# The order of VectorE's work in the attention heads of a two-block transformer kernel

## The chip, the cores and the metric

The kernel runs on one core of one Trainium2 chip. The metric is the device time of one execution in microseconds (us), as a median of several runs. All arithmetic is in 32-bit floats. TensorE (PE) does the matrix products and transposes, VectorE (DVE) and ScalarE (ACT) the elementwise work, SyncE (SP) starts nearly all transfers, GpSimd (POOL) a few gathers and scatters at the end.

## The reference, cut to what matters

Two transformer blocks run one after the other on 512 tokens of width 1024. The first block is a feed-forward part, a mixer with 16 attention heads of width 64, and a second feed-forward part. The second block has a gated linear attention, a latent attention and a mixture of 64 experts. The change touches only the 16 heads of the first block's mixer: eight "stick-breaking" heads, then eight "forgetting" heads.

```python
z = einsum('bhqd,bhkd->bhqk', q, k) * scale                 # stick-breaking
log_keep = where(mask, log_sigmoid(-z), 0.0)
later = cumsum(log_keep, axis=3, reverse=True) - log_keep
w = where(mask, exp(log_sigmoid(z) + later), 0.0)

fq, fk = rms_norm(fox_q, g_q), rms_norm(fox_k, g_k)         # forgetting, per head
z = einsum('bhqd,bhkd->bhqk', fq, fk) * scale + log_f_cum_q - log_f_cum_k
p = softmax(where(causal mask, z, -inf), axis=-1)

out = w @ v   or   p @ v;   mixer output = heads @ w_o
```

## The kernel before, in words

Every engine has its own written-out program, and semaphores tie them together; there is no planner. Each engine works its instructions off in the order in which they are written, so an instruction whose wait isn't met holds back everything behind it on that engine. What follows is the stretch of the mixer (about 590 to 890 us of the profiled execution).

The 16 heads (h = 0 to 15) come in 8 pairs (p = h // 2). Pairs 0 to 3 are stick-breaking, pairs 4 to 7 forgetting. n = h + 1 is the next head. While head h is turned and multiplied with its values, the scores and weights of head n are made, and the projections of a later pair run on PE.

PE, for each head h: `turn(h)` transposes the weights of the head (10 tiles of 128 x 128, line 800) once they are there (`s_p`). `scores(h + 1)` makes the next head's scores in PSUM banks 0 to 2 (line 791); in a forgetting pair it waits for the normed queries and keys of the pair (`s_qn`). `head_out(h)` multiplies the turned weights with the values into bank 6 (line 818); it waits for both copies of the turned tiles. Then comes projection work. In an odd head it is `first_half(p + 2)`: queries and keys of pair p + 2 (line 767), and for a forgetting pair the sum of squares of the queries (line 840). In an even head it is `second_half(p + 1)`: for a forgetting pair the sum of squares of the keys (line 848), and then `values(p + 1)` into bank 6 (line 773). `values` may only start when VectorE has copied the head's output out of bank 6 (`s_o`). In heads 13 and 14 six blocks of the output projection (`mix`, line 858) take that place.

ScalarE, for each head: a copy of six turned tiles (line 1331), then the exponentials of the next head, `softplus_log` and `stick_weights` or `forget_exp` (line 1316, one activation for each of four row tiles, each as soon as its maximum is there), and the copies and square roots of the projections (`raw_out`, `deviation`, line 1299). The root of the queries of pair p + 1 comes at the end of the odd head before (it ends up beside the turn of head h), the root of its keys in the even head h itself.

VectorE, for each head (lines 1679 to 1708):

- `turned_out(h)`, lines 1640 and 1643: the copy of four turned tiles, which waits for the turn.
- `head_copy(h)`, line 1647: bank 6 to SBUF, which waits for `head_out(h)` (`s_pv`).
- `log_weights(n)`, lines 1609 to 1617: for a stick-breaking head n. It waits for ScalarE's logarithm, and its last step releases ScalarE's exponential, which releases `turn(n)`.
- `masked_max(n)`, lines 1624 and 1627: for a forgetting head n, four additions of the mask and four row maxima, each of which releases one activation on ScalarE.
- `forget_probs(n)`, lines 1631 and 1634: waits for the four activations, then a reciprocal and four scalings; releases `turn(n)`.
- `inverse(p + 1, m)`, line 1651: the reciprocal of the deviation of the queries (m = 0) or keys (m = 1), in place; waits for ScalarE's root.
- `normed(p + 1, m)`, line 1658: two products, one for each head of the pair; releases `scores` through `s_qn`.
- `forget_rows`, lines 1665 and 1667: extra rows of queries and keys, in odd heads.
- `mix_part(d)`, line 1672: in heads 13 and 14, adds a block of the output projection to the residual.

The two inversions and the two norms stand in the even heads 6, 8, 10 and 12 (pairs 4, 5, 6 and 7). Head 6 is even too, but its next head, 7, is still stick-breaking: there the order is head copy, `log_weights(7)`, `inverse(4, 0)`, `normed(4, 0)`, `inverse(4, 1)`, `normed(4, 1)`. In heads 8, 10 and 12 it is `inverse(p + 1, 0)`, `masked_max(n)`, head copy, `forget_probs(n)`, `normed(p + 1, 0)`, `inverse(p + 1, 1)`, `normed(p + 1, 1)`.

Of the kernel before, what the change touches and what calls it, by code (L numbers as in the profile page):

```python
# [131 lines left out]
def build(nc, a, out):  # L132
    ctx = ExitStack()
    with ctx:
# [20 lines left out]
        def const(name):  # L155
            at, n = CONST[name]
            return cst[:, at:at + n]

        def col(name, j=None):
            at, n = COLS[name]  # L160
            return cols[:, at:at + n] if j is None else cols[:, at + j:at + j + 1]
# [25 lines left out]
        N_PAIR = 8  # L187
# [254 lines left out]
        def unit_psum(n):  # L442
            b = 2 * (n % 4)
            _, _, m, wide, _ = UNITS[n]
            return ps[0:m, b:b + 2, 0:TOK // 2] if wide else ps[0:m, b, :]
# [199 lines left out]
        def _(pe):  # L645
# [272 lines left out]
            for n, (it, c0, m, wide, _) in enumerate(UNITS):  # L918
                if it != item:
                    if item >= 0:  # L920
                        pe.drain().then_inc(freed[2 + item], 1)
                    item = it
                    pe.wait_ge(filled[2 + it], u.take(2 + it, 1)[0] + 16)
                if n >= 4:

                    pe.wait_ge(s_p2c[n % 2], (n - 4) // 2 + 1)
                b = 2 * (n % 4)
                for k in range(KC):
                    if n == 0:
                        pe.wait_ge(s_hn, KC * 3 + k + 1)  # L930
                    flags = dict(start=(k == 0), stop=(k == KC - 1))
                    if wide is None:
                        t = n - 4
                        last = mm(ps[0:m, b, :], hT[:, k, TILE0[t]:TILE0[t] + m], w2(it)[:, k, :], **flags)
                    elif wide:
                        for g in range(2):
                            last = mm(ps[0:m, b + g, 0:264], w2(it)[:, k, c0:c0 + m], hT[:, k, g * 264:(g + 1) * 264], **flags)
                    else:
                        last = mm(ps[0:m, b, :], w2(it)[:, k, c0:c0 + m], hT[:, k, META:TOK], **flags)
                last.then_inc(s_p2, 1)  # L940
# [538 lines left out]
        def _(dve):  # L1479
# [5 lines left out]
            def link(ins):  # L1485

                ins.then_inc(vec_sem[0], 1)
                steps[0] += 1
                dve.wait_ge(vec_sem[0], steps[0])
# [114 lines left out]
            def z_tiles():  # L1604
                return [ps[:, b, at:at + P * (t + 1)] for t, (b, at) in enumerate(Z_AT)]

            def log_weights(h):
                dve.wait_ge(s_sp, h + 1)
                v.scalar_tensor_tensor(out=buf1[:, 0:768].rearrange("p (b n) -> p b n", b=2), in0=ps[:, 0:2, 0:384],
                                       scalar=0.0, in1=buf1[:, 0:768].rearrange("p (b n) -> p b n", b=2),  # L1610
                                       op0=ALU.max, op1=ALU.add)
                link(v.scalar_tensor_tensor(out=buf1[:, 768:TRI], in0=ps[:, 2, :], scalar=0.0, in1=buf1[:, 768:TRI],
                                            op0=ALU.max, op1=ALU.add))
                link(v.tensor_tensor_scan(buf2[:, ::-1], const("resets")[:, ::-1], buf1[:, ::-1], 0.0, ALU.mult, ALU.add))
                v.tensor_tensor(buf1[:, 0:768].rearrange("p (b n) -> p b n", b=2), ps[:, 0:2, 0:384],
                                buf2[:, 0:768].rearrange("p (b n) -> p b n", b=2), ALU.subtract)
                v.tensor_tensor(buf1[:, 768:TRI], ps[:, 2, :], buf2[:, 768:TRI], ALU.subtract).then_inc(s_zz, 1)

            def masked_max(h):
                dve.wait_ge(s_z, h + 1)  # L1620
                tiles = z_tiles()
                for t in (3, 2, 1, 0):
                    diag = tiles[t][:, t * P:(t + 1) * P]
                    last = v.tensor_tensor(diag, diag, const("after"), ALU.add)
                link(last)
                for t in (3, 2, 1, 0):
                    v.tensor_reduce(fox_s[:, t:t + 1], tiles[t], AX_X, ALU.max, negate=True).then_inc(s_mx, 1)

            def forget_probs(h):
                dve.wait_ge(s_e, 4 * (h - 7))  # L1630
                link(v.reciprocal(fox_s[:, 8:12], fox_s[:, 4:8]))
                for t in range(4):
                    b = buf2[:, TILE_AT[t]:TILE_AT[t] + P * (t + 1)]
                    last = v.tensor_scalar(b, b, fox_s[:, 8 + t:9 + t], None, ALU.mult)
                last.then_inc(s_p, 1)

            def turned_out(h):
                dve.wait_ge(s_pt, h + 1)
                if h < 8:
                    v.tensor_tensor(PT[:, 0:4, :], ps[:, 3, :].rearrange("p (b q) -> p b q", b=4),  # L1640
                                    const("strict_t").unsqueeze(1).to_broadcast([P, 4, P]), ALU.mult).then_inc(s_ptc, 1)
                else:
                    v.tensor_copy(PT[:, 0:4, :].rearrange("p b q -> p (b q)"), ps[:, 3, :]).then_inc(s_ptc, 1)

            def head_copy(h):
                dve.wait_ge(s_pv, h + 1)
                v.tensor_copy(oT[h % 2 * HD:(h % 2 + 1) * HD, h // 2:h // 2 + 1, :], ps[0:HD, 6:7, :]).then_inc(s_o, 1)  # L1647

            def inverse(p, m):
                dve.wait_ge(s_qstd, 2 * (p - 4) + m + 1)  # L1650
                link(v.reciprocal(eb[:, m, :], eb[:, m, :]))

            def normed(p, m):
                dve.wait_ge((s_qc, s_kc)[m], p + 1)
                g = (gqs[:, p - 4:p - 3], col("g_k", p - 4))[m]
                for hh in range(2):
                    rows = slice(hh * HD, (hh + 1) * HD)
                    last = v.scalar_tensor_tensor(out=(qF, kF)[m][p % 2][hh][0:HD, :], in0=raw[m][rows, :], scalar=g[rows, :],
                                                  in1=eb[rows, m, :], op0=ALU.mult, op1=ALU.mult)
                last.then_inc(s_qn, 1)  # L1660

            def forget_rows(p):
                if p < 6:
                    for hh in range(2):
                        v.memset(qF[p % 2][hh][HD:72, :], 1.0)
                for hh in range(2):
                    v.tensor_scalar(kF[p % 2][hh][HD:72, :], Fc, ident[0:8, 2 * (p - 4) + hh:2 * (p - 4) + hh + 1], None, ALU.mult)\
                        .then_inc(s_fm, 1)

            def mix_part(d):  # L1670
                dve.wait_ge(s_wo, d + 1)
                v.scalar_tensor_tensor(out=xT[:, d, META:TOK], in0=ps[:, 7 - (d % 3) % 2, :], scalar=gate[1][:, d:d + 1],
                                       in1=xT[:, d, META:TOK], op0=ALU.mult, op1=ALU.add).then_inc(s_wp, 1)
# [5 lines left out]
            for h in range(N_HEAD):  # L1679
                p, n = h // 2, h + 1  # L1680
                turned_out(h)
                if n < 8:
                    head_copy(h)
                    log_weights(n)
                if h % 2 == 0 and 4 <= p + 1 < N_PAIR:
                    inverse(p + 1, 0)
                if n >= 8:
                    if n < N_HEAD:
                        masked_max(n)
                    head_copy(h)  # L1690
                    if n < N_HEAD:
                        forget_probs(n)
                if h == 0:
                    dve.wait_ge(s_f1, 2)
                    link(v.scalar_tensor_tensor(out=fA, in0=fA, scalar=0.0, in1=fB, op0=ALU.max, op1=ALU.add))
                    link(v.memset(fB, 1.0))

                    link(v.tensor_tensor_scan(Fc, fB, fA, 0.0, ALU.mult, ALU.add))
                if h % 2 == 0 and 4 <= p + 1 < N_PAIR:
                    normed(p + 1, 0)  # L1700
                    inverse(p + 1, 1)
                    normed(p + 1, 1)
                if h % 2 and 4 <= p + 2 < N_PAIR:
                    forget_rows(p + 2)
                if h in (13, 14):
                    for d in range(3 * (h - 13), 3 * (h - 13) + 3):
                        mix_part(d)
# [14 lines left out]
            for n in range(0, len(UNITS), 2):  # L1722
# [5 lines left out]
                if n - 1 in GATE_PAIRS:  # L1728

                    h = GATE_PAIRS[n - 1]  # L1730
# [110 lines left out]
            for un in range(GH * NT):  # L1841
                h, t = un // NT, un % NT
# [248 lines left out]
```

## Time and profile before

| | |
|---|---|
| three runs | 2852.21, 2854.35, 2855.42 us; median 2854.35 us |
| the profiled execution | 2856.67 us, of which span 2854.9 us |
| mean granted TensorE clock | 0.939 of full speed |
| PE busy | 2518.7 us (88%) |
| DVE busy | 1047.9 us (37%) |
| ACT busy | 465.7 us (16%) |
| POOL busy | 179.6 us (6%) |
| DMA | 563.19 MB, mean 197 GB/s |

The span runs from the first to the last instruction. Busy shares are of the span; weight loads of PE overlap its products and are counted apart. The granted clock is the share of TensorE's full speed that the chip gave it; 1.00 is 2.4 GHz and 0.50 is 1.2 GHz. In the page's 40 slices the stretch of the heads is slices 9 to 12, where PE is at nine tenths or more in each slice, VectorE at three to five tenths.

### The profile page before, as it was taken

The page shows a single profiled execution, that of the slowest core. Times are in us where ns is not written, and L with a number is a line of the kernel's source. Part 1 is how long each engine was busy: PE and PEld are TensorE (multiplying, and loading weights), DVE is VectorE, ACT ScalarE, POOL GpSimd, SP SyncE. Part 2 cuts the span into 40 slices and gives each one's busy share as a digit, 9 for nine tenths or more (in the row PEclk, how much of TensorE's full clock was granted, in tenths as well). Part 3 has the DMA queues.
Part 4 walks back from the last instruction along what each step waited for, and adds up shares of the span by engine and source line. Part 5 has one row for each costly group of instructions (what it writes and reads, how often), then busy time and mean ns, then how long its engine had stood idle before and what let it go on. Part 6 is the DMA issues. An engine that isn't in the chain of part 4 may idle for free. (4 is left out here: it accounts for less than half of the span.)

```text
span 2854.9 us, 24606 instructions
## 1 busy us (share of the span) xinstructions
PE 2518.7 (88%) x9051; PEld 1170.1 (41%) x9051; DVE 1047.9 (37%) x1236; ACT 465.7 (16%) x732; POOL 179.6 (6%) x458
## 2 busy tenths in 40 slices
PE   8999999999998999999997798688888788878884
PEld 4444444465564444434444454333333233323331
DVE  3655530145462333310106633433333333333334
ACT  2000000155332000000102130011111111111111
POOL 0000000000000000000000000111111111111110
PEclk9999999999899999999998799799899989999997
DMA  7444534122101121413201000799999999999995
GB/s 269 147 147 147 175 129 105 33 51 61 49 1 59 59 88 59 120 41 90 86 19 64 0 8 30 310 413 417 411 412 407 411 406 404 410 405 413 403 413 222
DMA packets 182831, 563.19 MB, mean 197 GB/s; under 512 B 16864, under 2 KB 132848, under 8 KB 156544
## 3 DMA queue, kind: packets, MB, share of 16 engines
q1 hardware_dynamic: 172384, 554.10, 50.8%
q0 software_dynamic: 10400, 8.42, 1.0%
q8 instruction: 35, 0.57, 0.1%
q14 instruction: 12, 0.10, 0.0%
HBM read 567.19 MB, written 20.97 MB: 206 GB/s over the span
## 5 line engine op out<-in xcount | busy, mean ns | idle before, releaser
L1143 PE MATMUL ps<-slot,xT 128*64 128x512 f32 x2048 | 516.4, 663 | 164.6 <-DMA slot<-in_expert_w_up 163.9
L715 PE MATMUL ps<-hT,slot 128*128 128x512 f32 x1408 | 614.4, 597 | 13.0 <-ACT hT L1238 7.2
L715 PEld LDWEIGHTS ps<-hT,slot 128*128 128x128 f32 x1408 | 267.9, 192 | 351.0 <-issue 347.4
L1143 PEld LDWEIGHTS ps<-slot,xT 128*64 128x64 f32 x2048 | 155.6, 152 | 523.5 <-issue 304.5
L743 PE MATMUL ps<-big,slot 128*128 128x512 f32 x704 | 310.4, 601 | 12.0 <-DVE big L1565 6.2
L1974 DVE COPY hT<-ps 128x256 f32<-128x256 f32 x64 | 27.2, 425 | 632.0 <-PE ps L1151 632.0
L1162 PE MATMUL ps<-slot,hT 128*64 128x512 f32 x1024 | 235.6, 602 | 1.2 <-DVE hT L1974 1.2
L1965 DVE RECIPROCAL xT<-xT 64x512 f32<-64x512 f32 x64 | 214.1, 3345 | 2.2
L743 PEld LDWEIGHTS ps<-big,slot 128*128 128x128 f32 x704 | 135.7, 193 | 182.0 <-issue 169.0
L1561 DVE RECIPROCAL eb<-eb 128x512 f32<-128x512 f32 x44 | 147.5, 3353 | 1.5
L1559 DVE TENSOR_SCALAR eb<-eb 128x512 f32<-128x512 f32 x44 | 18.8, 427 | 331.8 <-ACT eb L1248 331.8
L1444 ACT ACTIVATE xT<-ps 64x512 f32<-64x512 f32 x64 | 37.8, 590 | 599.4 <-PE ps L1143 599.4
L1588 DVE SCALAR_TENSOR_TENSOR xT<-ps,small,xT 128x512 f32<-128x512 f32 x16 | 12.0, 751 | 296.5 <-PE ps L743 296.5
L1162 PEld LDWEIGHTS ps<-slot,hT 128*64 128x64 f32 x1024 | 68.8, 137 | 116.1 <-issue 111.9
L2028 POOL MEMSET spare<- 1x4 f32 x1 | 0.1, 91 | 1806.7 <-DVEq L463 1806.7
L1450 ACT ACTIVATE hT<-ps 64x512 f32<-64x512 f32 x128 | 75.7, 592 | 203.1 <-PE ps L1162 202.4
L767 PE MATMUL ps<-hT,slot 128*128 128x512 f32 x240 | 105.9, 597 | 0.0
L1248 ACT ACTIVATE eb<-ps 128x512 f32<-128x512 f32 x44 | 26.3, 597 | 419.4 <-PE ps L715 419.3
L1225 ACT ACTIVATE tmp<-xT 128x512 f32<-128x512 f32 (+1 forms) x32 | 20.1, 632 | 368.0 <-DVE xT L1588 327.9
L1125 PE MATMUL ps<-cst,xT 64*128 64x64 f32 x512 | 67.1, 272 | 7.5 <-DMA xT<-normed_tokens,tcol 7.5
L773 PE MATMUL ps<-slot,hT 128*128 128x128 f32 x512 | 61.8, 284 | 6.9 <-DVE big L1647 6.9
L767 PEld LDWEIGHTS ps<-hT,slot 128*128 128x128 f32 x240 | 44.8, 190 | 55.1 <-issue 55.1
(331 smaller groups left out, 2313.2 us busy)
## 6 DMA issues: line engine op xcount, KB each, us to landing
slot<-in_expert_w_gate SPq DMA_DIRECT2D x64, 2048.0 KB, 19.4
slot<-in_expert_w_up SPq DMA_DIRECT2D x64, 2048.0 KB, 22.7
slot<-in_expert_w_down SPq DMA_DIRECT2D x64, 2048.0 KB, 25.0
slot<-in_w_mod SPq DMA_DIRECT2D x18, 2048.0 KB, 8.0
slot<-in_w_gate SPq DMA_DIRECT2D x22, 1024.0 KB, 5.5
slot<-in_w_up SPq DMA_DIRECT2D x22, 1024.0 KB, 7.9
slot<-in_w_down SPq DMA_DIRECT2D x16, 1408.0 KB, 7.4
slot<-in_w_in SPq DMA_DIRECT2D x24, 512.0 KB, 6.4
```

Of the source, the lines that this page charges most:

```text
L715: last = mm(ps[:, 2 * j + g, :], w[:, g, k, j * P:(j + 1) * P], hT[:, k, META:TOK], start=(k == 0), stop=(k == KC - 1))
L743: last = mm(ps[:, down_bank(d), :], w[:, f, :], aT[:, f, :], start=(f == 0), stop=(f == FC - 1))
L767: last = mm(ps[:, bank, :], pair_w[p][:, k, m, :], hT[:, k, META:TOK], start=(k == 0), stop=(k == KC - 1))
L773: last = mm(ps[:, bank, t * P:(t + 1) * P], hT[:, k, META + t * P:META + (t + 1) * P], pair_w[p][:, k, 2, :], start=(k == 0), stop=(k == K ...
L1125: last = nc.tensor.transpose(ps[:, 4 + j, k * CAP:(k + 1) * CAP], xs[j].rearrange("p (m k) -> p k m", k=KC)[:, k, :], ident[0:CAP, 0:CAP])
L1143: last = mm(ps[g * CAP:(g + 1) * CAP, j, :], xsT[j][:, k, :], w[g][:, k, :], start=(k == 0), stop=(k == KC - 1))
L1162: last = mm(ps[g * CAP:(g + 1) * CAP, 2 + j, :], hid[j][:, c, :], w[:, c, g * 512:(g + 1) * 512], start=(c == 0), stop=(c == 3))
L1444: av(sg[j], ps[0:CAP, j, :], ACT.Exp, scale=-1.0).then_inc(s_eg, 1)
L1450: last = av(ys[j][:, g * 512:(g + 1) * 512], ps[g * CAP:(g + 1) * CAP, 2 + j, :], ACT.Copy)
L1561: v.reciprocal(eb[:, j, :], eb[:, j, :]).then_inc(s_vec, 1)
L1965: v.reciprocal(sg[j], sg[j]).then_inc(s_vec, 1)
L1974: v.tensor_copy(hid[j].rearrange("p c s -> p (c s)"), ps[:, 6 + j, 0:4 * CAP]).then_inc(s_hd, 1)
```

## The change

In the loop over heads on VectorE, three things move. No instruction is added, dropped or resized, and the other engines' programs are the same.

1. In head 6, `inverse(4, 0)` and `normed(4, 0)` (one reciprocal and two products) are issued in front of `head_copy(6)` and `log_weights(7)`. They stood behind them.
2. In heads 8, 10, 12 and 14, `head_copy(h)` is issued in front of `masked_max(n)`. It stood between `masked_max(n)` and `forget_probs(n)`.
3. `inverse(p + 1, 0)` stands at the head of the loop body; in heads 8, 10 and 12 it is where it was, behind `turned_out(h)`.

Odd heads, and head 15, are as before.

```diff
             for h in range(N_HEAD):
                 p, n = h // 2, h + 1
                 turned_out(h)
+                if h % 2 == 0 and 4 <= p + 1 < N_PAIR:
+                    inverse(p + 1, 0)
+                if h == 6:
+                    normed(4, 0)
                 if n < 8:
                     head_copy(h)
                     log_weights(n)
-                if h % 2 == 0 and 4 <= p + 1 < N_PAIR:
-                    inverse(p + 1, 0)
-                if n >= 8:
+                elif h % 2 == 0:
+                    head_copy(h)
+                    masked_max(n)
+                    forget_probs(n)
+                else:
                     if n < N_HEAD:
                         masked_max(n)
                     head_copy(h)
...
                 if h % 2 == 0 and 4 <= p + 1 < N_PAIR:
-                    normed(p + 1, 0)
+                    if h != 6:
+                        normed(p + 1, 0)
                     inverse(p + 1, 1)
                     normed(p + 1, 1)
```

## Rows read from the trace of the kernel before

**Rows 1.** Waits of PE, 590 to 900 us: total us, times, longest.
```profile
PE ps L773 <- DVE big L1647: 6.9, 3, 2.3
PE ps L791 <- DVE slot L1658: 6.4, 1, 6.4
```

**Rows 2.** Timeline, heads 6 and 7: start, duration, engine, line, [idle before <- releaser].
```profile
692.55 0.69 ACT L1299 ACTIVATE eb<-ps,eps_col 128x512 f32<-128x512 f32 x1
...
696.79 0.68 DVE L1647 COPY big<-ps 64x512 f32<-64x512 f32 x1 [3.99 <-PE ps L818]
...
697.64 7.31 PE L773 MATMUL ps<-slot,hT 128*128 128x128 f32 x64
...
700.95 0.96 DVE L1609 SCALAR_TENSOR_TENSOR big<-ps,big 128x768 f32<-128x768 f32 x1 [3.49 <-ACT big L1306]
...
706.88 3.34 DVE L1651 RECIPROCAL eb<-eb 128x512 f32<-128x512 f32 x1
...
708.31 2.01 PE L800 MATMUL ps<-cst,big 128*128 128x128 f32 x10 [3.36 <-ACT big L1310]
...
715.18 1.51 DVE L1658 SCALAR_TENSOR_TENSOR slot<-tmp,cols,eb 64x512 f32<-64x512 f32 x2
...
716.74 4.64 PE L791 MATMUL ps<-slot 72*128 72x128 f32 x8 [6.42 <-DVE slot L1658]
...
721.31 4.53 PE L818 MATMUL ps<-big 128*64 128x128 f32 x20
```

**Rows 3.** Timeline, heads 8 and 9.
```profile
742.94 3.35 DVE L1651 RECIPROCAL eb<-eb 128x512 f32<-128x512 f32 x1 [0.48 <-ACT eb L1299]
...
743.82 2.40 PE L818 MATMUL ps<-big 128*64 128x128 f32 x20
...
746.15 1.13 PE L848 MATMUL ps<-eb,cst 128*128 128x512 f32 x2
746.32 0.89 DVE L1624 TENSOR_TENSOR ps<-ps,cst 128x128 f32<-128x128 f32 x4
...
748.85 0.67 DVE L1647 COPY big<-ps 64x512 f32<-64x512 f32 x1
...
749.58 9.04 PE L773 MATMUL ps<-slot,hT 128*128 128x128 f32 x64 [2.30 <-DVE big L1647]
...
756.48 1.51 DVE L1658 SCALAR_TENSOR_TENSOR slot<-tmp,cols,eb 64x512 f32<-64x512 f32 x2
...
759.87 2.32 PE L791 MATMUL ps<-slot 72*128 72x128 f32 x8
```

**Rows 4.** Timeline, heads 10 to 13.
```profile
788.24 7.41 PE L773 MATMUL ps<-slot,hT 128*128 128x128 f32 x64 [2.30 <-DVE big L1647]
...
795.14 1.51 DVE L1658 SCALAR_TENSOR_TENSOR slot<-tmp,cols,eb 64x512 f32<-64x512 f32 x2
...
796.90 2.33 PE L791 MATMUL ps<-slot 72*128 72x128 f32 x8
...
825.28 8.80 PE L773 MATMUL ps<-slot,hT 128*128 128x128 f32 x64 [2.30 <-DVE big L1647]
...
832.18 1.51 DVE L1658 SCALAR_TENSOR_TENSOR slot<-tmp,cols,eb 64x512 f32<-64x512 f32 x2
...
835.34 2.32 PE L791 MATMUL ps<-slot 72*128 72x128 f32 x8
```

**Rows 5.** Windows: length, busy of PE, PEld, DVE, ACT, POOL, then PEclk, DMA share, GB/s.
```profile
716.74:725.80 9.06, 9.06 (x29) 6.44 (x29) 3.25 (x9) 2.14 (x8) 0.00 (x0) 0.50 0.62 245
749.73:753.10 3.37, 3.37 (x17) 3.37 (x18) 2.87 (x8) 2.36 (x5) 0.00 (x0) 0.50 0.00 0
788.24:791.65 3.41, 3.41 (x30) 3.41 (x31) 2.78 (x7) 2.52 (x6) 0.00 (x0) 1.00 0.02 5
```

**Rows 6.** Timeline, head 14, PE and DVE.
```profile
856.00 10.57 PE L858 MATMUL ps<-big,slot 128*128 128x512 f32 x24
...
859.73 0.75 DVE L1672 SCALAR_TENSOR_TENSOR xT<-ps,small,xT 128x512 f32<-128x512 f32 x1 [0.64 <-PE ps L858]
```

## The prediction

> **What bounds the kernel now.** I read the page first. PE is busy for 88% of the span and VectorE for 37%, so as a whole VectorE sets nothing. But the change sits in the heads, and there the question is at which places PE stands still for VectorE. The page's chain of waits is of no use for that: it holds only the last steps of the kernel. The view that answers is PE's waits between 590 and 900 us. Two lines of it name VectorE: `values` (L773) waits three times for the head copy (L1647), 6.9 us in total, and `scores` (L791) waits once, 6.4 us, for a normed operand (L1658) [rows 1]. These are the four waits that the change aims at, 13.3 us in all. Then the timeline, to see what stands before each of them on VectorE.
>
> In heads 6 and 7 PE has finished `values(4)` at 697.64 + 7.31 = 704.95 us, waits 3.36 us for the last stick-breaking weights, turns them, and then waits 6.42 us until 716.74 for the normed keys of pair 4, which VectorE delivers at 715.18 + 1.51 = 716.69 [rows 2]. VectorE does two reciprocals and two norms in a row from 706.88 on, while before, until 696.79, it sat idle for 3.99 us.
>
> In heads 8, 10 and 12 PE stands for 2.30 us each before `values` [rows 3, 4]. In head 8 `head_out` ends at 743.82 + 2.40 = 746.22, yet the copy starts only at 748.85, because the mask and the maxima (from 746.32) are ahead of it. Everything PE does in this stretch outside the named waits is back to back, so a microsecond taken from PE's path here is one of the whole: what follows (feed-forward part, second block) starts from PE's end of it.
>
> The windows show a second price, the clock. PE ran at 0.50 (1.2 GHz) from 716.74 to 725.80, through all of `scores(8)` and `head_out(7)`, and for 3.4 us after the 2.3 us stop in head 8, but stayed at 1.00 (2.4 GHz) after the same stop in head 10 [rows 5]. Head 12's `values` took 8.80 us against 7.41 in head 10 [rows 4], so I read it as a fall too: two of three stops of 2.30 us were followed by the low clock.
>
> **Head 6: queries normed early.** Two instruction groups move from behind `log_weights(7)` to ahead of the head copy. `inverse(4, 0)` can start when ScalarE's root is there, 692.55 + 0.69 = 693.24; VectorE is free from 696.79 - 3.99 = 692.80. It ends at 693.24 + 3.34 = 696.58, the norm at 698.09, the head copy at 698.77 instead of 697.47 [rows 2]. So the copy is 1.3 us late and `values(4)` with it: it ends at 706.2 instead of 704.95. The cover is the 3.36 us wait for the stick-breaking weights, which arrive at 708.31 whatever PE does: `log_weights(7)` waits for ScalarE until 700.95 and VectorE is free at 698.8. Cost on the path: 0 (1.3 if that cover were gone). The SP queue refills a slot when `values(4)` ends, 1.3 us later, with weights that are used pairs later; no one waits for it.
>
> Behind the chain only the keys are left: 706.88 + 3.34 + 1.51 = 711.73, so `scores(8)` can start at 711.8 instead of 716.74. The turn of head 7 ends at 710.32, which is the next limit and lies below. Gain: 4.9 us. What is late next is still the normed keys, by 1.5 us. The clock is low there now and I expect it low again, since PE stands idle 2.1 us before the turn and 1.5 us behind it: 0 taken. Bounds: if it stays up, `scores(8)` and `head_out(7)` take 2.32 and 2.40 instead of 4.64 and 4.53 [rows 2, 3], 4.45 us more gain; if it rises later than now, up to 1 us is lost in the projection behind.
>
> **Heads 8, 10, 12: head copy first.** What goes: the 2.30 us before `values`. The copy can start at 746.3, when `head_out` has ended and `inverse(5, 0)` too (742.94 + 3.35 = 746.29), ends at 747.0, and PE is busy with L848 until 747.28 [rows 3]. So `values` starts without a stop, at 747.28. What is paid: the copy used to lie under ScalarE's exponentials; now mask, maxima, exponentials, scalings and the norms behind them all move back by its 0.67 us. The last of them releases the scores of the next head, and there the cover is thin:
>
> - Head 8: keys normed at 757.99 before, 758.66 now. The scores ran at 759.87 [rows 3]. They now start at 758.66: gain 1.21.
> - Head 10: keys normed at 796.65, now 797.32; scores at 796.90 before [rows 4]. Loss 0.42.
> - Head 12: 833.69, now 834.36; scores at 835.34 before. Gain 0.98.
>
> Sum 1.77 us of the 6.9 that seemed to be there. The rest becomes a new stop. With `values` at the full-clock 7.41 us, PE ends it in head 8 at 754.69. The turn in between takes 1.25 (before: end of `values` 758.62, scores 759.87), so PE could start the scores at 755.94 and stands until 758.66: 2.72 us. The same sum gives 2.72 in head 10 and 2.71 in head 12. VectorE is now the bound of the even heads.
>
> That new stop is longer than the 2.30 us ones and sits before `scores` and `head_out`, so a fall of the clock now costs there. No row shows this stop. Lower bound of its price: 0 per head. Upper bound: both instruction groups wholly at the low clock, 4.45 us, as in head 7 [rows 2]. A fall in `values` cost 9.04 - 7.41 = 1.63 and 8.80 - 7.41 = 1.39 us [rows 3, 4]. The rows nearest in kind are those of head 7, the nearest in length of stop are those of `values`; I take 2.5 us for each of three heads, 7.5 in all.
>
> The Trainium skill ("TensorE: Matmul & The Clock Gate", section "A second HAM failure mode: psum-queue depth-cycling") says that short pauses between groups of matmuls, met again at each turn through the PSUM banks, are enough to make the clock drop and recover over and over. It speaks against this change. By that rule all three new stops bring a fall; by this trace's two in three, two of them do: the sum at 2.5 each would be -0.8 or +1.7 us. The trace agrees that stops of 2.30 us suffice, though not each time.
>
> **Head 14.** The copy waits for `head_out(14)`, which ends at 856.0; before, mask and maxima went first. From the mask's start to the end of the probabilities is at most 757.99 - 746.32 - 1.51 - 3.35 - 1.51 = 5.3 us [rows 3], so they end by 856.7 + 5.3 = 862.0, under the 10.57 us of `mix`. `mix_part` (0.75) would end at 862.8; the third block of `mix`, which needs its bank, starts at 856.00 + 2/3 x 10.57 = 863.05 [rows 6]. Cost 0; 0.3 if that cover fails. The early `inverse` of point 3 of the change moves nothing in heads 8 to 12.
>
> **Sum.** 4.9 + 1.8 - 7.5 = -0.8, a loss of 0.8 us against the profiled execution: span 2854.9 + 0.8 = 2855.7, plus 1.8 around it, 2857.5. That execution lies 2.3 us above the median of the three runs, which spread over 3.2 us; on the median's scale the forecast is 2854.35 + 0.8 = 2855.2 us. What a measurement can tell from no change is about 0.2%, 5.7 us, so this is "the same".
>
> **Rivals.** (a) *The clock stays up.* If PE's new stops are not followed by low stretches, all 6.7 us are gained: 2847.7. With head 7's low stretch gone too, 2843.2. For it: head 10. Against it: heads 8 and 12, with shorter stops. Partly so (falls costing under 1 us in all) gives over 5.7 us. (b) *The new stop costs its full price*, the slower end. In heads 9, 11 and 13 scores and head output run wholly at 1.2 GHz: 3 x 4.45 = 13.35 against 6.7, so 6.65 us slower, 2861.0. It decides from 2.2 us a head on, where the gain is eaten; slower by over 0.2% it is from 4.1 us a head. For it: head 7, the one case in which this very pair of groups followed a wait for normed operands. Against it: the stop there was 6.42 us with another before it. By the skill's rule named above this is the case to expect. (c) *The copy is not the limit.* If `head_out` and `inverse` end later than the rows say, `values` still stands; then heads 8 to 12 give 1.77 less and only the stop moves, about 2849 to 2857. For it: copy and PE are within 0.1 us of each other. (d) *Head 6 pays.* The late `values(4)` reaches the turn: 1.3 of the 4.9 is lost, about 2856.5; the 2.1 us left speak against it.
>
> **How the numbers follow.** The forecast, with a clock price between 1 and 12.4 us in all, which takes in (c) and (d): 0.70, all within 0.2%. (a) 0.14, faster. (b) 0.16, slower. The range reaches from (a) without head 7, 2847.7, to (b), 2861.0, rounded outwards by half a microsecond for the spread of runs: 2847 to 2861.5. What is left out, clock up in head 7 as well or low longer than 4.45 us allows, and luck of the runs, I put at 0.18.
>
> **What would show it.** `scores(8)` starts about 15 us after the head output of head 6 has ended (696.8), not 20 as before. No wait of `values` for L1647 is left in heads 8 to 12; a new wait of L791 for L1658 of 2.7 us stands in heads 9, 11 and 13, and from the start of L848 to those scores it is 12.5 us in each. The window over scores and `head_out` there has a granted clock under 1.00. The forecast is wrong if those windows are at 1.00 throughout, or if L791's stops are short because the norms don't move back by 0.67.

## The result and the profile after

The changed kernel takes 2859.98 us (median of 22 runs, 2856.0 to 2862.96) against 2854.65 us before (22 runs, 2852.1 to 2857.45): ratio 1.0017, 95% interval 1.0011 to 1.0024. That is 5.3 us slower by the medians (the ratio makes it 4.9), just under the 0.2% (5.7 us) that I had called "the same", and it is a real difference: the interval leaves 1 out. The profiled execution has a span of 2856.2 us and a mean granted clock of 0.936.

Waits of PE after, 590 to 900 us (total us, times, longest), to be read against [rows 1]:

```profile
PE ps L791 <- DVE slot L1658: 9.8, 4, 2.7
PE ps L773 <- DVE big L1647: 1.0, 1, 1.0
```

The 6.9 us before `values` in heads 8, 10 and 12 are gone. Of the 6.4 us before `scores(8)`, 1.6 are left, but three new waits of 2.7 us stand in the same line.

Timeline after, heads 6 to 9 (start, duration, engine, line, [idle before <- releaser]), against [rows 2 to 4]:

```profile
690.78 1.02 PE L840 MATMUL ps<-eb,cst 128*128 128x512 f32 x2
...
699.65 7.41 PE L773 MATMUL ps<-slot,hT 128*128 128x128 f32 x64 [1.02 <-DVE big L1647]
709.14 1.94 PE L800 MATMUL ps<-cst,big 128*128 128x128 f32 x10 [2.08 <-ACT big L1310]
712.64 4.64 PE L791 MATMUL ps<-slot 72*128 72x128 f32 x8 [1.56 <-DVE slot L1658]
717.21 3.70 PE L818 MATMUL ps<-big 128*64 128x128 f32 x20
...
734.67 1.02 PE L840 MATMUL ps<-eb,cst 128*128 128x512 f32 x2
...
742.16 7.37 PE L773 MATMUL ps<-slot,hT 128*128 128x128 f32 x64
749.63 1.31 PE L800 MATMUL ps<-cst,big 128*128 128x128 f32 x10
753.69 4.34 PE L791 MATMUL ps<-slot 72*128 72x128 f32 x8 [2.75 <-DVE slot L1658]
```

VectorE in head 8 after: inverse, copy, mask, and the last norm (the maxima, probabilities and second inverse between them are left out):

```profile
737.99 3.35 DVE L1651 RECIPROCAL eb<-eb 128x512 f32<-128x512 f32 x1 [0.48 <-ACT eb L1299]
741.38 0.68 DVE L1647 COPY big<-ps 64x512 f32<-64x512 f32 x1
741.99 0.88 DVE L1624 TENSOR_TENSOR ps<-ps,cst 128x128 f32<-128x128 f32 x4
...
752.12 1.51 DVE L1658 SCALAR_TENSOR_TENSOR slot<-tmp,cols,eb 64x512 f32<-64x512 f32 x2
```

Windows after, over scores, head output and nothing else in heads 9 and 11; head 13 has the same (length, then busy of PE, PEld, DVE, ACT, POOL, then the granted clock, DMA share, GB/s):

```profile
753.69:761.68 7.99, 7.99 (x28) 5.52 (x28) 3.12 (x9) 1.96 (x8) 0.00 (x0) 0.57 0.00 0
794.53:802.53 8.00, 8.00 (x28) 5.55 (x28) 3.13 (x9) 2.08 (x8) 0.00 (x0) 0.57 0.00 0
```

PE never pauses in these windows and yet needs 8.0 us for what took 4.6 before (759.87 to 764.45). A granted clock of 0.57 means that most of that time it had 1.2 GHz.

To compare traces I use two distances. "Heads" is from the start of the last sum of squares before head 6 (L840, 690.78 here, 689.96 before) to the start of the turn of head 15 (L800, 869.86 here, 866.40 before). "Behind" is from there to the first router product (L1089, 1774.7 here, 1769.3 before), the end of the attention parts of the second block. Heads: 176.4 us before, 179.1 after, 2.6 more. Behind: 902.9 before, 904.8 after, 1.9 more, in a part that the change doesn't touch. What follows, from the router product to the end, says nothing about a change of a few microseconds: it took 1081.5 to 1085.6 us in the thirteen traces, and 1085.6 and 1081.7 in the two of the kernel before.

### The profile page after: what moved, and what is told of

It is laid out like the page before. It is cut to its first block and busy times, and to the rows that moved or that the text cites. A ratio compares the mean times of both kernels' runs of the same rounds, so it can differ in the third digit from the quotient of the medians.

```text
span 2856.2 us, 24606 instructions
## 1 busy us (share of the span) xinstructions
PE 2529.1 (89%) x9051; PEld 1175.7 (41%) x9051; DVE 1047.3 (37%) x1236; ACT 465.8 (16%) x732; POOL 179.7 (6%) x458
## 5 line engine op out<-in xcount | busy, mean ns | idle before, releaser
L1143 PE MATMUL ps<-slot,xT 128*64 128x512 f32 x2048 | 519.4, 666 | 159.6 <-DMA slot<-in_expert_w_up 158.7
L743 PEld LDWEIGHTS ps<-big,slot 128*128 128x128 f32 x704 | 135.9, 194 | 182.0 <-issue 168.9
L1225 ACT ACTIVATE tmp<-xT 128x512 f32<-128x512 f32 (+1 forms) x32 | 20.1, 632 | 369.1 <-DVE xT L1588 328.1
L2033 POOL DMA_INDIRECT xT<-normed_tokens,tcol x66 | 64.3, 974 | 34.0 <-issue 34.0
```

Of the source, the lines that this page charges most:

```text
L743: last = mm(ps[:, down_bank(d), :], w[:, f, :], aT[:, f, :], start=(f == 0), stop=(f == FC - 1))
L1143: last = mm(ps[g * CAP:(g + 1) * CAP, j, :], xsT[j][:, k, :], w[g][:, k, :], start=(k == 0), stop=(k == KC - 1))
L2033: pool.indirect_dma_start(xs[j], None, u_dram, bass.IndirectOffsetOnAxis(tcol[j][:, :], 0), bounds_check=SEQ - 1, oob_is_err=False).then_i ...
```

## The experiments

The kernel before was timed beside each group of runs (2854.71, 2855.25 and 2854.89 us). Ratios are to it. In the table, "scores" is from L840 of the odd head to the scores behind the next turn, in heads 8/9, 10/11 and 12/13.

| kernel | median us | ratio (95%) | heads | scores | behind |
|---|---|---|---|---|---|
| before | 2854.65 | 1 | 176.4 | 20.3, 18.6, 20.0 | 902.9 |
| after | 2859.98 | 1.0017 (1.0011 to 1.0024) | 179.1 | 19.0, 19.0, 19.0 | 904.8 |
| e1_queries_early | 2846.66 | 0.9970 (0.9959 to 0.9982) | 169.2 | 18.6, 20.1, 18.6 | 904.6 |
| e2_copy_first | 2861.41 | 1.0022 (1.0013 to 1.0031) | 183.2 | 19.0, 19.0, 19.0 | 903.1 |
| e3_fill_new_stop | 2847.35 | 0.9974 (0.9963 to 0.9984) | 169.1 | 19.0, 19.0, 19.0 | 904.4 |
| e4_split_norm | 2848.97 | 0.9977 (0.9968 to 0.9987) | 168.9 | 17.4, 17.4, 17.4 | 904.9 |
| e5_split_fill | 2848.10 | 0.9974 (0.9964 to 0.9984) | 163.7 | 17.4, 17.4, 17.4 | 909.8 |
| e6_fill_all | 2836.91 | 0.9934 (0.9920 to 0.9947) | 159.9 | 17.4, 17.4, 17.4 | 902.5 |
| e7_fill_mask_first | 2848.54 | 0.9974 (0.9964 to 0.9983) | 169.1 | 21.0, 21.1, 19.5 | 904.3 |
| e8_copy_on_scalar | 2839.12 | 0.9944 (0.9930 to 0.9957) | 158.7 | 17.0, 17.0, 17.0 | 904.6 |
| e9_later_arrival | 2857.09 | 1.0010 (1.0001 to 1.0019) | 180.0 | 19.0, 19.0, 19.0 | 902.9 |

The distances are of one profiled execution each, the medians of several. Taken against the kernel before, heads and behind together come within 1 us of the change of the median in every row but three: e1 (5.6 us faster by the distances, 8.0 by the median), e3 (5.9 and 7.3) and e9 (3.6 slower and 2.4). What these three owe to the part behind the router product, or to executions other than the profiled one, stays open.

### The two parts alone

e1_queries_early, on the kernel before:

```diff
                 turned_out(h)
+                if h == 6:
+                    inverse(4, 0)
+                    normed(4, 0)
                 if n < 8:
...
-                if h % 2 == 0 and 4 <= p + 1 < N_PAIR:
+                if h % 2 == 0 and 4 < p + 1 < N_PAIR:
                     inverse(p + 1, 0)
...
-                    normed(p + 1, 0)
+                    if h != 6:
+                        normed(p + 1, 0)
```

> Only the head 6 part of the change (queries of pair 4 inverted and normed ahead of the head copy); heads 8 to 14 as before. Theory (the clock takes back what the copy gives): scores(8) starts 4.9 us earlier relative to head 6 and its low-clock stretch is about as long as before, so 5 to 6 us faster than before, ratio about 0.998; heads 8 to 13 keep three stops of 2.3 us before the values. Rival (head 6 pays): the values of pair 4, late by 1.3 us or more, reach the turn of head 7, gain under 4 us.

Measured: 8.0 us faster. Of that its trace has 7.3 in the heads: the expected 4.9 us (scores(8) 21.85 us after L840, before 26.78), 0.8 in `head_out(7)` (3.72 against 4.53), and 1.5 because in its execution only one of three `values` ran into the low clock instead of two. Behind the heads it loses 1.7 again. The rival is out: `values(4)` comes 1.2 us late and the wait for the weights shrinks to 2.07.

e2_copy_first, on the kernel before:

```diff
                 if n >= 8:
+                    if h % 2 == 0:
+                        head_copy(h)
                     if n < N_HEAD:
                         masked_max(n)
-                    head_copy(h)
+                    if h % 2:
+                        head_copy(h)
```

> Only the other part: head copy ahead of mask and maxima in heads 8, 10, 12 and 14; head 6 as before. Theory: 1.8 us earlier score starts against 3 x 3.4 us of scores and head output at the low clock, so some 8 to 11 us slower than before (ratio 1.003 to 1.004), with three stops of 2.7 us before the scores and a granted clock of 0.50 for some 6.8 us after each. Rival (the loss came from elsewhere, the late norms or the second half of the kernel): within 3 us of before.

Measured: 6.7 us slower, and just as much in the heads. All three score starts come at 19.0 us as worked out, and in each the clock falls, for 6.8, 3.4 and 6.8 us. So the second part alone is the slower one. The two parts don't add up: -8.0 + 6.7 would be 1.3 us faster, and together they are 5.3 slower. In the heads the gap is 3.2 us (-7.3 and +6.7 against +2.6), and it is the clock: the fall in `values` that e1 happens to lose (1.5 us) is taken away by the copy's part too and can't be gained twice, and in e2 the middle stretch is half as long, so that scores and head output there take 6.32 us where the changed kernel needs 8.00 (1.7 us). The other half of the gap shows neither in the heads nor behind them, and stays open.

### Is it the clock or VectorE?

e3_fill_new_stop, on the changed kernel:

```diff
                 turn(h)
+                if h in (9, 11, 13):
+                    pe.wait_ge(s_qstd, 2 * (p - 3) + 2)
+                    for k in range(3):
+                        mm(ps[:, 7, :], const("ident"), hT[:, k, META:TOK], start=True, stop=True)
                 if h + 1 < N_HEAD:
                     scores(h + 1)
```

> The changed kernel with three extra products (identity by a tile of hT, 128x512, into the idle bank 7, never read) on PE between the turn and the scores in heads 9, 11 and 13: PE is busy for 2.6 of the 2.7 us in which it stood, and the scores start no earlier or later. It adds work that the result doesn't need. Theory (clock): granted clock 1.00 in scores and head output, each head 3.4 us shorter, 10.3 us in all: about 2850, and 5 us faster than before. Rival (VectorE's later norms are the loss, the low clock only goes with them): as slow as the changed kernel, about 2860.

Measured: 2847.35 us, 12.6 below the changed kernel. Timeline of this kernel in head 9 and the window over its scores and head output (the timeline counts each of these products twice, so x6 is three):

```profile
748.30 2.74 PE L881 MATMUL ps<-hT,cst 128*128 128x512 f32 x6
751.21 2.42 PE L791 MATMUL ps<-slot 72*128 72x128 f32 x8 [0.17 <-DVE slot L1662]
753.56 2.40 PE L818 MATMUL ps<-big 128*64 128x128 f32 x20
```

```profile
751.21:755.90 4.69, 4.69 (x29) 3.44 (x29) 2.74 (x8) 0.58 (x1) 0.00 (x0) 1.00 0.00 0
```

The scores start no earlier (19.0 us in all three heads), VectorE works as in the changed kernel, and useless work stands where PE was idle. All that differs is the clock, and the heads are 10.0 us shorter; 0.4 more are gained behind them, and 2.2 of the 12.6 lie in neither. This is what shows the cause: the low clock behind the new stops costs 10 us in the heads, and VectorE's later norms cost nothing beyond their place in the sum.

e4_split_norm gives the first head of a pair its operands first (each norm now counts by itself in `s_qn`, and ScalarE's wait for it is doubled to match):

```diff
-                pe.wait_ge(s_qn, 2 * (p - 4) + 2)
+                pe.wait_ge(s_qn, 4 * (p - 4) + (3 + hh if p == 4 else 2 + 2 * hh))
...
                     if h != 6:
-                        normed(p + 1, 0)
+                        normed(p + 1, 0, (0,))
                     inverse(p + 1, 1)
-                    normed(p + 1, 1)
+                    normed(p + 1, 1, (0,))
+                    if h != 6:
+                        normed(p + 1, 0, (1,))
+                    normed(p + 1, 1, (1,))
```

> The changed kernel with the norms of each pair's second head (two products of 0.75 us) moved behind those of the first, which alone the next scores need. The keys of the first head are there 1.5 us earlier, the stop before the scores is 1.2 us instead of 2.7. Theory (clock): 3 x 1.5 us from the stops (and 0.75 in head 7), and the clock stays at 1.00 after so short a stop, 10.3 us more: about 2845, 9 to 10 us faster than before. Rival (the low clock would come with any stop, or isn't what costs): only 4.5 to 5.3 us better than the changed kernel, about 2855.

Measured: 2848.97 us, 11.0 below the changed kernel, 4 us short of the theory. Head 9 of this kernel:

```profile
752.62 2.42 PE L791 MATMUL ps<-slot 72*128 72x128 f32 x8 [1.10 <-DVE slot L1658]
754.97 4.07 PE L818 MATMUL ps<-big 128*64 128x128 f32 x20
```

The scores come 1.6 us earlier, as expected. But after a stop of only 1.1 us the clock still fell, this time during the head output, which took 4.07 us instead of 2.40, in all three heads (low for 3.4 us each). My expectation that the clock stays up after so short a stop was wrong.

e5_split_fill is e4 with one such product in heads 9, 11 and 13; e6_fill_all has three more in head 7:

```diff
+                if h == 7:
+                    pe.wait_ge(s_qstd, 2)
+                    for k in range(2):
+                        mm(ps[:, 7, :], const("ident"), hT[:, k, META:TOK], start=True, stop=True)
                 turn(h)
+                if h in (7, 9, 11, 13):
+                    pe.wait_ge(s_qstd, 2 * (p - 3) + 2)
+                    mm(ps[:, 7, :], const("ident"), hT[:, 0, META:TOK], start=True, stop=True)
```

> e4_split_norm with one extra product (128x512, never read) before the scores in heads 9, 11 and 13, to fill the 1.1 us stop that was still followed by 3.4 us of low clock. Theory: the last three low stretches go (5 us against e4), scores start 1.6 us earlier than in e3_fill_new_stop: about 2843. Rival: a 1.1 us stop isn't the cause, the low clock comes with the scores' narrower products themselves: 2848 to 2849 as e4.

> e5_split_fill with three more extra products in head 7, two between the values of pair 4 and the turn and one before the scores, so that PE isn't idle there for more than 0.4 us. Theory: the ten microseconds of low clock in heads 7 and 8 go as well, 4 to 4.5 us better than e5: about 2838.5. Rival: the fall there stems from the 1.0 us stop before the values or the turn, and stays: as e5.

In the heads both do what was expected: e5 has no low stretch left in heads 9 to 13 (163.7 us, 5.2 less than e4), e6 none at all (159.9 us, 3.8 less than e5; expected were 4 to 4.5). e6 is the fastest version, 18 us below the kernel before and 1.6 below what was expected. The window of e6 over heads 7 to 14, and the one of the changed kernel:

```profile
705.00:840.00 135.00, 133.30 (x658) 85.99 (x657) 80.01 (x141) 51.44 (x100) 0.00 (x0) 1.00 0.13 44
```

```profile
705.00:843.00 138.00, 125.82 (x583) 84.28 (x582) 74.84 (x131) 49.65 (x98) 0.00 (x0) 0.89 0.12 43
```

The time of e5 doesn't follow: 2848.10 us, 5 more than expected. Of its 5.2 us from the heads 4.9 are lost again behind them, 909.8 us against 904.9. Four low stretches there are longer than in e4: those that start at 1221.6, 1392.3 and 1634.6 us last 10.2 us where e4's last 6.8, and the one that lasts 44.3 us in e4 lasts 47.8 and has another of 6.8 us in front of it, from 1528.8 us on. e6, which reaches the same work 3.3 us earlier than e5, has none of this: its part behind the heads is 7.3 us shorter.

### Which order is right once the clock is held

e7_fill_mask_first is e6 with `masked_max(n)` in front of `head_copy(h)` in the even heads again.

> e6_fill_all with the old order in heads 8, 10, 12 and 14 again (mask and maxima, then the head copy). Theory (with the clock held up, the copy-first order is worth having): the 2.3 us stops before the values return, PE takes 18.6 to 18.7 us from the last sum of squares of an odd head to the scores of the next, against 17.4 in e6, and may fall to the low clock in the values again (1.5 us a head): 4 to 8 us slower than e6, about 2841 to 2845. Rival (order in the even heads doesn't matter, all of e6's gain is from the filled stops and the split norm): within 1.5 us of e6.

Measured: 11.6 us slower than e6, 9.2 of them in the heads. The stops of 2.3 us before `values` are back, two of the three `values` took 8.95 and 9.04 us, and the extra product before the scores now fills no stop but costs its 0.86 us. That last part (2.6 us in all) is my design's fault and not the order's; I hadn't counted it. Of the remaining 6.6 us in the heads one half is the two falls (8.95 and 9.04 against 7.36 us), the other the stops themselves: with the clock held behind it, copy first is the better order, by 3.3 us from the stops alone.

e8_copy_on_scalar takes `head_copy` off VectorE in heads 8, 10 and 12 (and the extra products out of heads 9, 11 and 13 of e6). On VectorE the copy then stays in head 14 alone; this edit isn't shown here:

```diff
                 elif n < N_HEAD:
+                    if h in (8, 10, 12):
+                        act.wait_ge(s_pv, h + 1)
+                        av(oT[0:HD, h // 2:h // 2 + 1, :], ps[0:HD, 6:7, :], ACT.Copy).then_inc(s_o, 1)
                     forget_exp(n)
```

> e6_fill_all with the head copies of heads 8, 10 and 12 on ScalarE, ahead of its exponentials, so that they delay neither mask nor norms on VectorE; no extra products in heads 9, 11 and 13. Theory: the stop before the scores is 1.1 - 0.67 = 0.4 us, the clock stays up, 3 x 0.6 us better in the heads than e6: about 2835. Rival: ScalarE's copy delays the first exponential by more than the copy takes, or the unfilled 0.4 us is still followed by the low clock: slower than e6 by 1 to 5 us.

In the heads it is 1.2 us shorter than e6, less than the expected 1.8, with a stop of 0.7 us instead of 0.4; the clock stays at 1.00. The whole time is 2839.12 us, 2.2 above e6 rather than below: behind the heads it has a low stretch near 1682 us that e6 hasn't (904.6 against 902.5). The two distances leave 0.9 of the 2.2 us, and the rest lies within the spread of the five runs of each. ScalarE pays a little, too: its table load comes behind the copy, and in head 8 the first exponential starts 1.84 us after the mask, in e6 1.63.

### Where the other microseconds are

r_before and r_after are second profiled executions of the two kernels, unchanged.

> The kernel before once more, unchanged, for a second look at its low-clock stretches. Theory: starts of work are the same to a tenth of a microsecond; the three 2.30 us stops before the values are again followed by the low clock in some heads and not in others, at 1.4 to 1.6 us each. Rival: the falls belong to fixed heads (8 and 12, not 10).

> The changed kernel once more, unchanged. Theory: the three 2.7 us stops before the scores are all followed by the low clock again, and scores with head output take 7 to 9 us instead of 4.7. The median of its 22 runs lies 2 us above the execution that was profiled, so a stretch of the heads longer than the first one's 179.1 us would explain it. Rival: the falls come in only some heads, and the other microseconds lie outside the heads.

For the kernel before the rival was right, that the falls have fixed places. For the changed kernel all three falls came again, but not a longer stretch of the heads. The kernel before had its low stretches in heads 8 and 12 again and at the same distance from L840 within 0.2 us, and 176.5 us in the heads; the changed kernel again had 179.1 us, with all three falls. From 360 us to the router product every low stretch came again, in both kernels, at the same distance from L840 within 0.2 us. So in this part where the clock falls is not luck of an execution: it is the kernel's own, and shifts when its times shift. In the first 50 us it is not so: around 40 us the clock was low for 6.8 us in one execution of the kernel before and for 10.2 in the other. Heads 8 and 12 are no property of these heads either, since in e1 it was head 10.

The heads explain 2.6 of the 5.3 us. Behind them the windows show a low stretch that both profiled executions of the changed kernel have and neither of the kernel before. First the changed kernel, then the kernel before at the same work, the transposes behind the latent attention (L1068) and the first products after them (L1073):

```profile
1702.90:1706.20 3.30, 3.17 (x10) 2.44 (x11) 0.00 (x0) 1.11 (x2) 0.00 (x0) 0.51 0.46 159
```

```profile
1698.70:1702.00 3.30, 3.16 (x14) 2.00 (x15) 0.00 (x0) 1.98 (x2) 0.00 (x0) 1.00 0.42 159
```

What this stretch costs can be read from the same two traces, from the starts of the transposes (L1068) before it and behind it. Before it they start at 1698.84 us in the kernel before and 1703.03 in the changed one, 4.2 us apart. Behind it, first the kernel before, then the changed one, they are 5.8 us apart:

```profile
1713.48 1.04 PE L1068 MATMUL ps<-cst,xT 128*128 128x128 f32 x8
```

```profile
1719.30 1.04 PE L1068 MATMUL ps<-cst,xT 128*128 128x128 f32 x8
```

So the stretch costs 1.6 us. The distance "behind" had already grown by 0.7 us ahead of it and shrinks by 0.4 us after it, where low stretches that both kernels have begin at slightly other work or end earlier; together that is the 1.9.

e9_later_arrival asks whether that depends on when the stage is reached:

```diff
                 p = h // 2
+                if h == 15:
+                    mm(ps[:, 3, :], const("ident"), hT[:, 0, META:TOK], start=True, stop=True)
                 turn(h)
```

> The changed kernel with one extra product (128x512, never read) before the turn of head 15, so that everything behind the heads comes 0.86 us later and nothing in heads 7 to 14 changes. It asks where the part of the slowdown comes from that isn't in the heads: both traces of the changed kernel have a low-clock stretch near 1703 us (in the latent attention) that neither trace of the kernel before has. Theory (that stretch depends on when the stage is reached): it is gone, as in e2_copy_first, which arrives 4.1 us later than the changed kernel, and the time is 1 us below the changed kernel's in spite of the added work. Rival (the stretch belongs to the changed kernel's order): it stays, 0.9 us slower than the changed kernel.

Measured: 2857.09 us, 2.9 below the changed kernel's 2859.98 although it does more; 1 us was expected. The heads are 1.0 us longer (the extra product is in them), the part behind them 1.9 us shorter (902.9, as before), so the trace accounts for the expected 1 us and not for the rest. The window at the same work shows the full clock:

```profile
1703.80:1707.10 3.30, 3.06 (x14) 1.90 (x15) 0.00 (x0) 1.88 (x2) 0.00 (x0) 1.00 0.43 159
```

So of the slowdown 1.9 us are the clock behind the heads, 1.6 of them a fall 830 us behind their end that comes or goes with a shift of 0.9 us. In the table every kernel has one of a few values behind the heads, 902.5 to 903.1, 904.3 to 904.9, or 909.8 in e5. What is left, 0.8 us of the medians' 5.3, lies within the spread of executions (5 to 7 us); I didn't settle it.

## Why the prediction was right, and what was wrong in it

- *Queries normed early, 4.9 us.* Right: scores(8) comes 21.86 us after L840 instead of 26.78, 4.92 less. `values(4)` is late (1.2 us, estimated 1.3) and the wait for the weights takes it up. The low stretch there stayed, as taken; it ended earlier within `head_out(7)`, 0.8 us more gain, inside the bounds given.
- *Copy first, 1.21, -0.42, 0.98.* Right: 1.23, -0.40, 1.01 (20.25, 18.61, 20.02 against 19.02, 19.01, 19.01). The mask starts 0.61 us behind the copy's start, and everything behind it moved by that.
- *The new stop, 2.72 us.* Right: 2.75, 2.74, 2.73.
- *Its price, 2.5 us a head, 7.5 in all.* Mis-sized. From the start of the scores to the start of the projections it is 7.99, 8.00, 7.99 against 4.58, 4.59, 4.58: 3.41 a head, 10.2 in all. I had lowered the price of head 7's rows because its stops were longer, and leaned on the 1.5 us of a fall in `values`; but the length of the stop hardly mattered (1.1 us was enough in e4), and the clock stayed low twice as long as behind a stop before `values` (6.8 us against 3.4). The sum for the heads is then 4.92 + 0.83 + 1.84 - 10.23 = -2.64, which is the measured 179.08 - 176.44.
- *"A microsecond taken from PE's path here is one of the whole."* Wrong, the step that failed. It holds for work and not for the clock: 1.9 us were lost behind the heads, 1.6 of them in one low stretch at 1703 us, and the sum had no term for that.
- *The signs.* They came as named: `scores(8)` starts 15.1 us after the head output of head 6 has ended, the scores of heads 9, 11 and 13 stand 12.5 us behind the start of L848, and the granted clock over scores and head output is 0.57.
- *Head 14.* Nothing lost: from the turn of head 14 to that of head 15 it is 16.08 us in both.
- *The rivals.* (a), no falls, did not come; e3 shows what it would have been, 7.4 us faster than before, close to the 6.7 of the sum. (b), the full price, was nearer than my middle: 10.2 of its 13.35 us. (c) and (d) were not seen.

The sign was called rightly (0.8 us slower, measured 5.3) and the time lies in the range, but the centre was 4.8 us too low. In the heads the sum missed by 1.8 us: 2.7 too little for the falls, against 0.8 gained in `head_out(7)` that it had put at nothing. Another 1.9 lay behind the heads. That the time stayed within 0.2% of before, as the 0.70 wanted, was luck: 0.4 us more and it would have been outside. Rival (b) and its side should have had more than 0.16. The Trainium skill ("TensorE: Matmul & The Clock Gate", section "A second HAM failure mode: psum-queue depth-cycling") has it that short pauses between groups of products make the clock drop again and again; the trace after agrees, with three stops and three falls; e3 and e8, with stops of 0.2 and 0.7 us in their place, have none.

## What to carry to other kernels

Before taking a wait from one place, work out where the same engine will wait next and what it runs behind that wait: this change removed 6.9 us of stops and put 8.2 us of others in front of scores and head outputs, where a fall of TensorE's clock cost 3.4 us each. Where a stop can't be removed, products nobody reads are a cheap cover (nine of them in e3, three to a stop, took 10.0 us out of the heads). And with an engine whose clock falls at places that shift with the program, a trace comparison must be made stage by stage over the whole kernel: part of the effect can sit far from the change, and two edits needn't add up.

## What was not expected of the hardware

- Stops as short as 1.10 us, with the scores behind them, were followed by the low clock in three heads of three (e4), while a stop of 2.30 us before `values` wasn't in one of three (head 10 before and in r_before). A stop of 1.04 us before `values(4)` in e6 wasn't either, so the length of a stop alone doesn't tell. With stops of 0.7 us (e8) and 0.2 us (e3) the clock stayed at 1.00.
- The places of the falls in the heads repeat between executions of one kernel: 749.7 and 824.8 us in one, 751.0 and 826.1 in the other, whose L840 came 1.24 us later.
- A shift of 0.9 us decided on a low stretch 830 us later (e9).
- PE working without a pause did not bring the full clock back soon: in head 7 before it was busy for all of 9.06 us at 0.50 [rows 5].
